# Dense channel mixer of a hybrid decoder: plain fp32 products from a six-slot weight ring in place of high and low parts

## What is computed

```
def swiglu(x, wg, wu, wd):
    return (jax.nn.silu(x @ wg) * (x @ wu)) @ wd
...
hp = hp + swiglu(rmsnorm(hp, norm_g[layer, 1]), ffn_w_gate[f], ffn_w_up[f], ffn_w_down[f])
hs = hs + swiglu(rmsnorm(hs, norm_g[layer, 1]), ffn_w_gate[f], ffn_w_up[f], ffn_w_down[f])
```

## Time and profile before

| what | before |
|---|---|
| median of 3 runs | 2461.19 us (2452.08 to 2462.34) |
| profiled execution, its own time | 2464.63 us |
| span of that execution | 2462.8 us |
| mean granted TensorE clock | 0.903 |
| PE busy | 2159.2 us (88%) |
| DVE busy | 1315.7 us (53%) |
| ACT busy | 1067.0 us (43%) |
| DMA, mean | 180 GB/s, 443.24 MB |

### The profile page before, as it was taken

How to read it: one execution, slowest core, us unless ns; L and a number is a source line. 1 busy time by engine, 2 the same in 40 slices (tenths; PEclk the granted TensorE clock), 3 DMA queues, 4 the chain that set the end, 5 groups by cost and what they waited for, 6 DMA issues and landing times. The chain is left out here.

```text
span 2462.8 us, 38086 instructions
## 1 busy us (share of the span) xinstructions
PE 2159.2 (88%) x15542; PEld 1740.0 (71%) x15543; DVE 1315.7 (53%) x1913; ACT 1067.0 (43%) x1688; POOL 143.0 (6%) x176
## 2 busy tenths in 40 slices
PE   6986997799976898888878887699999999999997
PEld 4765996699954675577644454588778787787876
DVE  4125233444313465326733231488888888788885
ACT  3112321333213455224442330267666766667664
POOL 5001140000003100100000000000000000000000
PEclk8997998899988888856889998799999999999998
DMA  5100002554285542203024323489999999999993
GB/s 196 69 1 18 20 21 91 171 165 154 76 254 218 201 158 68 33 1 137 1 111 171 155 110 69 144 288 355 337 319 321 335 329 338 329 324 332 326 338 114
DMA packets 309634, 443.24 MB, mean 180 GB/s; under 512 B 60855, under 2 KB 273031, under 8 KB 306256
## 3 DMA queue, kind: packets, MB, share of 16 engines
q1 hardware_dynamic: 305706, 373.53, 46.1%
q0 software_dynamic: 3456, 67.11, 6.7%
q10 hardware_dynamic: 294, 0.11, 0.0%
HBM read 435.35 MB, written 13.67 MB: 182 GB/s over the span
## 5 line engine op out<-in xcount | busy, mean ns | idle before, releaser
L2763 DVE TENSOR_TENSOR moe.w_gate_up_lo<-mw.w_gate_up,moe.w_gate_up_hi 128x2048 fp32r<-128x2048 f32 x176 | 402.6, 2291 | 121.5 <-ACT moe.w_gate_up_hi L2696 121.3
L2696 ACT CAST moe.w_gate_up_hi<-mw.w_gate_up 128x2048 fp32r<-128x2048 f32 x176 | 335.7, 1909 | 161.5 <-PE moe.b L1050 161.5
L1048 PE MATMUL moe.b<-moe.w_gate_up_hi,moe.x_block_hi 128*128 128x512 f32 x704 | 277.3, 394 | 0.0
L1050 PE MATMUL moe.b<-moe.w_gate_up_hi,moe.x_block_lo 128*128 128x512 f32 x704 | 275.5, 391 | 0.0
L1049 PE MATMUL moe.b<-moe.w_gate_up_lo,moe.x_block_hi 128*128 128x512 f32 x704 | 275.1, 391 | 0.0
L2702 ACT CAST moe.w_down_hi<-mw.w_down 128x1024 fp32r<-128x1024 f32 x176 | 185.2, 1052 | 94.6 <-PE moe.b L1050 79.1
L2763 DVE TENSOR_TENSOR moe.w_down_lo<-mw.w_down,moe.w_down_hi 128x1024 fp32r<-128x1024 f32 x176 | 208.1, 1218 | 18.0 <-ACT moe.w_down_hi L2702 18.0
L1048 PE MATMUL moe.b<-moe.w_down_hi,moe.hidden_t_hi 128*128 128x512 f32 x352 | 148.6, 422 | 21.2 <-issue 18.8
L1050 PEld LDWEIGHTS moe.b<-moe.w_gate_up_hi,moe.x_block_lo 128*128 128x128 f32 x704 | 132.7, 188 | 28.5
L1048 PEld LDWEIGHTS moe.b<-moe.w_gate_up_hi,moe.x_block_hi 128*128 128x128 f32 x704 | 133.1, 189 | 26.3
L1049 PEld LDWEIGHTS moe.b<-moe.w_gate_up_lo,moe.x_block_hi 128*128 128x128 f32 x704 | 133.0, 189 | 26.2
(11 more groups left out here) (615 smaller groups left out, 4187.0 us busy)
## 6 DMA issues: line engine op xcount, KB each, us to landing
mw.w_gate_up<-in_moe_w_gate SPq DMA_DIRECT2D x176, 512.0 KB, 5.9
mw.w_gate_up<-in_moe_w_up SPq DMA_DIRECT2D x176, 512.0 KB, 7.2
mw.w_down<-in_moe_w_down SPq DMA_DIRECT2D x176, 512.0 KB, 6.0
rin.w_rkv<-in_rw_w_rkv SPq DMA_DIRECT2D x3, 4096.0 KB, 18.2
ffn.w<-in_ffn_w_gate SPq DMA_DIRECT2D x11, 1024.0 KB, 5.4
ffn.w<-in_ffn_w_up SPq DMA_DIRECT2D x11, 1024.0 KB, 8.0
ffn.w<-in_ffn_w_down SPq DMA_DIRECT2D x10, 1024.0 KB, 6.0
out_win_kv_sample<-in_state_win_kv SPq DMA_DIRECT2D x1, 8128.0 KB
```

What stands on the lines that cost most here:

```text
L1048: nc.tensor.matmul(out, w_hi, x_hi, start=start, stop=False)
L1050: return nc.tensor.matmul(out, w_lo, x_hi, start=False, stop=stop)
L2696: nc.scalar.copy(gu_hi[:, j % HR], M.wgu[:, j % M.RGU]).then_inc(gu_high, 1)
L2763: return nc.vector.tensor_tensor(out, x, high, ALU.subtract)
```

## The change

The high and low parts go, and with them `split`, `low`, `hidden_low` and `wait_used` in this stage. Each call of `product` becomes one fp32 matmul that reads the weight slot and the normed x or the hidden rows as they are. The ring gets six slots in place of two, all of them issued by `ahead` inside the norm's block; SP reloads a slot when the products that read it are counted, and PE waits for a slot's DMAs itself. The hidden rows of all 22 chunks are kept in fp32. The down products run over the banks in another order, beginning with bank 4, and in the first group wait for the last hidden chunks one by one. The experts keep their high and low parts.

The diff, with the lines left out that only restate this:

```diff
-        xn, xh, xl = s.sb("xn", [P, DC, NT]), s.sb("xn_hi", [P, DC, NT], F32R), s.sb("xn_lo", [P, DC, NT], F32R)
-        RING, ROWS = 2, 4
+        xn = s.sb("xn", [P, DC, NT])
+        RING, ROWS = 6, 4
         ND = -(-FC // ROWS)
         W = s.sb("w", [P, RING, 2 * DC * GW])
-        WH, WL = (s.sb(n, [P, 2, 2 * DC * GW], F32R) for n in ("w_hi", "w_lo"))
-        HH, HL = (s.sb(n, [P, FC, NT], F32R) for n in ("hidden_hi", "hidden_lo"))
-        silu_b, H = s.sb("silu", [P, 2, NT]), s.sb("hidden", [P, 2, NT])
+        H, silu_b = s.sb("hidden", [P, FC, NT]), s.sb("silu", [P, 2, NT])
         bank = [s.bank(f"b{i}") for i in range(8)]
         w_in = [s.sem(f"w_in{i}") for i in range(RING)]
-        xhi, xlo, high, ready, used = (s.sem(n) for n in ("x_high", "x_low", "w_high", "w_ready", "down_groups_used"))
-        mm, silu, raw, hhi, hid, down, added = (s.sem(n) for n in (
-            "products", "silu", "hidden_raw", "hidden_high", "hidden", "down", "added"))
+        xr, mm, silu, hid, used, down, added = (s.sem(n) for n in (
+            "x_ready", "products", "silu", "hidden", "down_groups_used", "down", "added"))
         count = lambda j: FC - ROWS * j if j == ND - 1 else ROWS
...
-        size = lambda n: 2 * DC * GW if n < NG else count(n - NG) * D
...
+        slot = lambda n: W[:, n % RING, 0:2 * DC * GW if n < NG else count(n - NG) * D]
...
-        stage_norm(nc, G, "norm1", C_NG + 8, xn, lambda sp: [load(sp, n) for n in range(RING)], H, bank[0])
+        stage_norm(nc, G, "norm1", C_NG + 8, xn, lambda sp: [load(sp, n) for n in range(RING)], H[:, 0:2], bank[0])
         with nc.Block() as block:
             @block.sync
             def _(sp):
                 for n in range(RING, NG + ND):
-                    sp.wait_ge(ready, n - RING + 1)
+                    if n - RING < NG:
+                        sp.wait_ge(mm, 2 * (n - RING) + 2)
+                    else:
+                        sp.wait_ge(used, n - RING - NG + 1)
                     load(sp, n)
 
             @block.tensor
             def _(pe):
-                pe.wait_ge(xlo, 1)
+                def arrived(n):
+                    pe.wait_ge(w_in[n % RING], 32 * (n // RING + 1))
+
                 for f in range(FC):
                     n = f // 2
                     if f % 2 == 0:
-                        pe.wait_ge(ready, n + 1)
+                        arrived(n)
                     if f >= 4:
-                        pe.wait_ge(raw, f - 3)
-                    hi, lo = (t.rearrange("p (x k n) -> p x k n", x=2, k=DC) for t in (WH[:, n % 2], WL[:, n % 2]))
+                        pe.wait_ge(hid, f - 3)
+                    w = slot(n).rearrange("p (x k n) -> p x k n", x=2, k=DC)
                     for x in range(2):
                         for k in range(DC):
-                            cols = slice(P * (f % 2), P * (f % 2) + P)
-                            last = product(nc, bank[2 * (f % 4) + x][:, 0:NT], hi[:, x, k, cols], lo[:, x, k, cols],
-                                           xh[:, k, :], xl[:, k, :], k == 0, k == DC - 1)
+                            last = nc.tensor.matmul(bank[2 * (f % 4) + x][:, 0:NT], w[:, x, k, P * (f % 2):P * (f % 2) + P], xn[:, k, :],
+                                                    start=(k == 0), stop=(k == DC - 1))
                     last.then_inc(mm, 1)
-                pe.wait_ge(hid, FC)
                 for j in range(ND):
                     n = NG + j
-                    pe.wait_ge(ready, n + 1)
-                    hi, lo = (t[:, 0:size(n)].rearrange("p (k n) -> p k n", n=D) for t in (WH[:, n % 2], WL[:, n % 2]))
-                    for c in range(DC):
+                    arrived(n)
+                    w = slot(n).rearrange("p (k n) -> p k n", n=D)
+                    for i in range(DC):
+                        c = (2 * (FC % 4) + i) % DC
+                        if j == 0 and i % 2 == 0:
+                            pe.wait_ge(hid, FC - 3 + i // 2)
                         for k in range(count(j)):
-                            f, cols = ROWS * j + k, slice(P * c, P * c + P)
-                            last = product(nc, bank[c][:, 0:NT], hi[:, k, cols], lo[:, k, cols],
-                                           HH[:, f, :], HL[:, f, :], f == 0, f == FC - 1)
+                            f = ROWS * j + k
+                            last = nc.tensor.matmul(bank[c][:, 0:NT], w[:, k, P * c:P * c + P], H[:, f, :],
+                                                    start=(f == 0), stop=(f == FC - 1))
                         if j == ND - 1:
                             last.then_inc(down, 1)
                     if j < ND - 1:
...
-                def split(n):
-                    act.wait_ge(w_in[n % RING], 32 * (n // RING + 1))
-                    wait_used(act, n)
-                    nc.scalar.copy(WH[:, n % 2, 0:size(n)], W[:, n % RING, 0:size(n)]).then_inc(high, 1)
-
...
                 for f in range(FC):
                     act.wait_ge(mm, f + 1)
                     if f >= 2:
-                        act.wait_ge(raw, f - 1)
+                        act.wait_ge(hid, f - 1)
                     nc.scalar.activation(silu_b[:, f % 2, :], bank[2 * (f % 4)][:, 0:NT], ACT.Silu).then_inc(silu, 1)
...
-                def low(n):
-                    dve.wait_ge(high, n + 1)
-                    w = W[:, n % RING, 0:size(n)]
-                    wait_used(dve, n)
-                    nc.vector.tensor_tensor(WL[:, n % 2, 0:size(n)], w, WH[:, n % 2, 0:size(n)], ALU.subtract).then_inc(ready, 1)
-
...
+                    nc.vector.tensor_tensor(H[:, f, :], silu_b[:, f % 2, :], bank[2 * (f % 4) + 1][:, 0:NT], ALU.mult).then_inc(hid, 1)
+                for i in range(DC):
+                    c = (2 * (FC % 4) + i) % DC
+                    dve.wait_ge(down, i + 1)
                     nc.vector.tensor_tensor(G.h[:, c, :], G.h[:, c, :], bank[c][:, 0:NT], ALU.add).then_inc(added, 1)
```

More of the change, by code:

```diff
@@ L1056, in stage_ffn @@
     with Scope(nc, "ffn") as s:
-        xn, xh, xl = s.sb("xn", [P, DC, NT]), s.sb("xn_hi", [P, DC, NT], F32R), s.sb("xn_lo", [P, DC, NT], F32R)
-        RING, ROWS = 2, 4
+        xn = s.sb("xn", [P, DC, NT])
+        RING, ROWS = 6, 4
         ND = -(-FC // ROWS)
         W = s.sb("w", [P, RING, 2 * DC * GW])
-        WH, WL = (s.sb(n, [P, 2, 2 * DC * GW], F32R) for n in ("w_hi", "w_lo"))
-        HH, HL = (s.sb(n, [P, FC, NT], F32R) for n in ("hidden_hi", "hidden_lo"))
-        silu_b, H = s.sb("silu", [P, 2, NT]), s.sb("hidden", [P, 2, NT])
+        H, silu_b = s.sb("hidden", [P, FC, NT]), s.sb("silu", [P, 2, NT])
         bank = [s.bank(f"b{i}") for i in range(8)]
         w_in = [s.sem(f"w_in{i}") for i in range(RING)]
-        xhi, xlo, high, ready, used = (s.sem(n) for n in ("x_high", "x_low", "w_high", "w_ready", "down_groups_used"))
-        mm, silu, raw, hhi, hid, down, added = (s.sem(n) for n in (
-            "products", "silu", "hidden_raw", "hidden_high", "hidden", "down", "added"))
+        xr, mm, silu, hid, used, down, added = (s.sem(n) for n in (
+            "x_ready", "products", "silu", "hidden", "down_groups_used", "down", "added"))
         count = lambda j: FC - ROWS * j if j == ND - 1 else ROWS
-        size = lambda n: 2 * DC * GW if n < NG else count(n - NG) * D
[L1072 to L1077, removed]
+        slot = lambda n: W[:, n % RING, 0:2 * DC * GW if n < NG else count(n - NG) * D]
         def load(sp, n):
-            slot, sem = W[:, n % RING, 0:size(n)], w_in[n % RING]
+            sem = w_in[n % RING]
             if n < NG:
                 for i, name in enumerate(("ffn_w_gate", "ffn_w_up")):
-                    sp.dma_start(slot.rearrange("p (x k n) -> p x k n", x=2, k=DC)[:, i],
+                    sp.dma_start(slot(n).rearrange("p (x k n) -> p x k n", x=2, k=DC)[:, i],
                                  io[name][0, :, GW * n:GW * n + GW].rearrange("(k p) n -> p k n", p=P)).then_inc(sem, 16)
@@ L1088, in load @@
                     h = count(n - NG) // 2
-                    sp.dma_start(slot.rearrange("p (k n) -> p k n", n=D)[:, h * i:h * i + h],
+                    sp.dma_start(slot(n).rearrange("p (k n) -> p k n", n=D)[:, h * i:h * i + h],
                                  io["ffn_w_down"][0, r + P * h * i:r + P * h * i + P * h, :].rearrange("(k p) n -> p k n", p=P)) \
                         .then_inc(sem, 16)
-        stage_norm(nc, G, "norm1", C_NG + 8, xn, lambda sp: [load(sp, n) for n in range(RING)], H, bank[0])
+        stage_norm(nc, G, "norm1", C_NG + 8, xn, lambda sp: [load(sp, n) for n in range(RING)], H[:, 0:2], bank[0])
         with nc.Block() as block:
```

3 lines of the change are left out of this document (removed).

## The result

The changed kernel takes 2511.25 us (median of four runs, 2502.36 to 2522.94); the kernel before took 2459.5 us in the same comparison (2452.08 to 2462.34). The ratio is 1.0213, with a 95% interval from 1.0167 to 1.0259: slower by 51.75 us. The forecast was 2512, by 51 us.

What follows compares the result with a forecast made beforehand. The stage was taken to be bound by TensorE's products, with splitting beside them; products at 258.5 us in place of 215.7 (+42.8) and a start 8.1 us later gave +50.9 us, so 2512 us, range 2490 to 2521 (its own 2503 to 2518).

Steps and rivals of the forecast that it cites:

- The price of the plain product: Mixer's products: 0.485 us a plain call, 528 calls 256.1 us, against 0.400 us for three split products, 211.3 us in all.
- Rival (b): Every mixer product: a plain one costs two records at the split pace, 0.267 us; 2397 us in all; chance 0.03.
- The start: Before the mixer's first product: SP issues twelve transfers inside the norm, so it starts at 467.9, not 459.8; 8.1 us lost.
- Rival (a): Mixer's start: SP's issues hold nobody up, PE starts at about 449.6; sum +32.6, 2494 us; chance 0.12.
- (c): Mixer's start: the first slot lands late because twelve transfers share the DMA engines; start at 476, 2520 us; chance 0.03.
- The pace of 2.96 us: SP's issues inside the norm: 2.96 us for each 1024 KB transfer, eight more ending at 467.5.
- The half clock: Mixer's first products: PE's clock is at 0.50 as before, a loss of 2.45 us, bounds 1.7 to 5.
- The gap between up and down: Between the up and down products: PE's gap of 2.1 us goes.
- no wait for weights: Mixer's product stretch: no new wait arises; each 2 MB slot is used for 15.5 us, asking 135 GB/s where 347 are shown.
- The sum: Whole stage: products +42.8 us and start +8.1 us, together +50.9 us, for a median of 2512 us.

Runs made afterwards that it cites:

- the later test there: Kernel before, with SP issuing only router weights and three half-slots inside the route stage's norm and nine transfers in the next block: 2459.43 us, ratio 0.9979.
- first experiment: Changed kernel, with SP issuing two of the six slots inside the norm and four at the head of the next block: 2487.97 us, ratio 1.0112.
- third experiment: Changed kernel, with a ring of two slots in place of six, both issued inside the norm: 2490.05 us, ratio 1.0113 to the kernel before.

## Why the prediction was right

- **The price of the plain product.** 0.485 us was read from another stage, and 0.485 is what the mixer shows. The stretch from the first to the last start is 732.1 - 473.24 = 258.9 us, to which the last record's 0.24 us belongs: 259.1, by the forecast 258.5. Rival (b) would have needed 0.267.
- **The start.** The forecast put the first product at 467.9 - 438.55 = 29.35 us after SP's first issue; it came at 29.79. Eight more issues took 472.79 - 448.70 = 24.1 us in place of 23.7, and 0.45 us lie between the last one and the first product in place of 0.44. Rival (a) falls with that, and (c) with the landing of the first slot at 451.7. The first four issues gave no warning of this in the kernel before, where they end long before the norm; the route stage did, and the later test there shows that the reading was right. The pace of 2.96 us was a middle of two stages' rows with no reason given for it; the last section shows what it goes with.
- **The half clock.** This term was a little too small. The clock is 0.50 for some 6.0 us, so 3.0 us are lost in place of the 2.45 that were kept from before, and 256.1 + 3.0 = 259.1 us are the measured stretch. In the kernels of the first and third experiment the same products have some 4.2 and 3.6 us at 0.50. What sets it these runs don't show; the bounds of 1.7 to 5 us of loss hold all of them.
- **The gap between up and down** went, and no wait for weights came, which the two-slot ring shows with less to spare.
- **The sum.** In the profiles, from SP's first issue to the last product: 288.65 - 236.75 = 51.9 us, forecast 50.9. Issued in time (first experiment) the same products would cost 269.1 - 236.75 = 32.3 us, where rival (a) had 32.6. That the median of the whole time came out within 1 us of the forecast is partly luck: its interval reaches from 41 to 64 us. What carries the account is the stage's own rows.

## What to carry to other kernels

Where PE is full, taking work from engines that run beside it gives nothing: what counts is the price of the form on PE, and it can be read from another stage of the same kernel with the same shape, as start-to-start distance at the same clock. Prefetching more is not free if the issuing engine has to finish before a common end of a block: count the issue time of the transfers beyond what the queue takes at once (here about 3 us for each further MB), and put them behind the block's end. A form that is dearer per product can still win where it needs no preparation: plain products filled the 10 us in which the split ones had to be made ready.

## What the runs showed of the hardware that was not expected

The part of the program outside the stage is the same in all these kernels but for the route edit, yet single executions differ there by more than the experiments' smaller effects. In the stretch ahead of the mixer, the changed kernel and the one with two slots ahead execute the same 5523 matmul records:

```profile
0.00:443.40 443.40, 367.56 (x5523) 300.10 (x5524) 152.73 (x258) 97.10 (x168) 84.96 (x119) 0.88 0.18 58
```

```profile
0.00:435.80 435.80, 359.86 (x5523) 296.82 (x5524) 152.31 (x258) 97.20 (x168) 85.59 (x119) 0.90 0.18 59
```

The first row is the changed kernel's, the second the other's: 7.6 us apart, with PE busy for 7.7 us more at a mean clock of 0.88 in place of 0.90. That a profiled execution lies some 10 us above its kernel's median can therefore come from stages that were not changed, which is why the steps above are read from the stage's own rows.

SP's issue of a transfer is not only a matter of its bytes: the same 1 MB took 0.38 us to issue as the first and 2.92 as the fifth. In the changed kernel the fourth issue ends at 445.89 + 2.81 = 448.70 and the first transfer lands at 443.45 + 5.2 = 448.65; the fifth ends at 448.74 + 2.92 = 451.66 and the second lands at 443.88 + 7.8 = 451.68. So it goes on: each issue from the fourth to the twelfth ends within some 0.2 us of the landing of the transfer three before it. In the kernel with two slots ahead, where SP paused, the seventh and eighth issue are of other lengths,

```profile
447.87 2.39 SPq L1073 DMA_DIRECT2D ffn.w<-in_ffn_w_gate  x1
450.31 4.38 SPq L1073 DMA_DIRECT2D ffn.w<-in_ffn_w_up  x1
```

and end at 450.26 and 454.69, where the fourth and fifth transfer land at 450.4 and 454.6. So with three of these transfers under way SP is held until one has landed, and its pace is theirs: 1 MB at the 348 GB/s of the stretch is 3.0 us. This is read from coinciding times; no run changed the size of these transfers.

Behind the gate and up transfers of the earlier trace rows, whose rows in memory are 1 KB long (256 columns of fp32), at 1.42 us for 512 KB, three of 512 KB with rows of 4 KB take 2.37 us together, 0.79 each. Whether their longer rows, or the room in the queue at that moment, make this difference was not tried.
